# Attention scores from high and low parts in three passes, and the place where the next pair's weights are split

## What is computed

```python
q_lat = jnp.einsum('bthn,lhn->bthl', q_nope, w_uk)
...
s = (jnp.einsum('bqhl,bkl->bhqk', ql, ckv) + jnp.einsum('bqhr,bkr->bhqk', qr, krope))
s = s.astype(jnp.float32) * ATTN_SCALE
mask = (qp[:, None] // CHUNK) >= k_chunk[None, :]
p = jax.nn.softmax(jnp.where(mask, s, -jnp.inf), axis=-1).astype(ckv.dtype)
return jnp.einsum('bhqk,bkl->bqhl', p, ckv)
```

## Time and profile before

| what | value |
|---|---|
| median of 3 runs | 1476.83 us (1472.91 to 1477.15) |
| profiled execution, its own time | 1476.03 us |
| its span, first to last instruction | 1474.0 us |
| TensorE matmul busy | 1278.2 us (87%) |
| VectorE busy | 532.4 us (36%) |
| ScalarE busy | 457.4 us (31%) |
| granted TensorE clock, mean | 0.936 of full speed |

### The profile page before, as it was taken

One profiled execution on the slowest core, in us unless ns is written; L12 is line 12 of the kernel. 1 busy time (PEld: TensorE's weight loads), 2 busy tenths in 40 slices (PEclk: granted clock), 3 DMA queues, 4 the chain that ended last, 5 costly groups with the idle time before them and its releaser, 6 DMA issues.

```text
span 1474.0 us, 22958 instructions
## 1 busy us (share of the span) xinstructions
PE 1278.2 (87%) x8602; PEld 706.5 (48%) x8603; DVE 532.4 (36%) x1057; ACT 457.4 (31%) x713; POOL 32.7 (2%) x40
## 2 busy tenths in 40 slices
PE   6999999999999988888887887788788888887785
PEld 4999999887767733232222222222232233222221
DVE  4335446275664342323222222232213232322233
ACT  5432334245443223232232222222222223222223
POOL 1000000000100000000000000000000000000000
PEclk9999999999999989999898899899889999998898
DMA  9554551132363479999999999999999999999996
GB/s 324 145 172 141 165 170 40 35 109 79 116 196 140 174 296 426 429 433 431 430 433 431 432 434 429 432 434 429 433 434 388 429 435 430 434 431 429 434 431 261
DMA packets 71112, 474.45 MB, mean 322 GB/s; under 512 B 9676, under 2 KB 46800, under 8 KB 56480
## 3 DMA queue, kind: packets, MB, share of 16 engines
q1 hardware_dynamic: 70144, 472.35, 78.5%
q0 software_dynamic: 688, 1.43, 0.3%
q10 hardware_dynamic: 240, 0.09, 0.0%
HBM read 470.49 MB, written 3.38 MB: 321 GB/s over the span
## 4 chain that ended last, share of the span: by engine, by line
PE 63%; DMA 26%; DVE 5%; issue 3%; ACT 3%; DVEq 0%; ACTq 0%; SPq 0%
DMA ring<-in_w_down 16%; PE ps L991 11%; PE ps L1010 8%; PE ps L679 5%; PE ps L680 5%; PE ps L681 5%; DMA gate_b<-in_w_up 4%; PE ps L965 4%; DVE hreg L1742 3%; PE ps L997 2%; DMA gate_b<-in_w_down 2%; DMA ring<-in_w_up 2%; PE ps L843 2%; PE ps L844 2%; PE ps L845 2%
## 5 line engine op out<-in xcount | busy, mean ns | idle before, releaser
L1742 DVE TENSOR_TENSOR hreg<-ps,hreg 128x512 f32<-128x512 f32 x264 | 160.9, 682 | 205.9 <-PE ps L1017 205.9
L991 PE MATMUL ps<-ring,cq 128*32 128x512 f32 x1600 | 185.0, 603 | 22.9 <-DVE hreg L1742 17.3
L1746 DVE TENSOR_TENSOR work<-work,ps 128x128 f32 x33 | 9.5, 288 | 449.9 <-PE ps L997 449.9
L679 PE MATMUL ps<-xT_hi,w_hi 128*128 128x320 f32 (+1 forms) x528 | 164.9, 312 | 0.6 <-DVE w_lo L1437 0.6
L680 PE MATMUL ps<-xT_lo,w_hi 128*128 128x320 f32 (+1 forms) x528 | 164.0, 311 | 0.0
L681 PE MATMUL ps<-xT_hi,w_lo 128*128 128x320 f32 (+1 forms) x528 | 163.9, 310 | 0.0
L1010 PE MATMUL ps<-ring,work 128*32 128x512 f32 x768 | 129.3, 835 | 20.6 <-DMA ring<-in_w_down 20.6
L1017 PE MATMUL ps<-krt,const 32*128 32x512 f32 x528 | 102.7, 626 | 29.7 <-ACT krt L1383 29.7
L991 PEld LDWEIGHTS ps<-ring,cq 128*32 128x32 f32 x1600 | 51.9, 111 | 134.5 <-issue 127.2
L1437 DVE TENSOR_TENSOR w_lo<-ring,w_hi 128x1024 fp32r<-128x1024 f32 (+1 forms) x66 | 76.8, 1205 | 107.6 <-ACT w_hi L1125 107.6
L1125 ACT CAST w_hi<-ring 128x1024 fp32r<-128x1024 f32 (+1 forms) x66 | 65.2, 1033 | 145.8 <-PE ps L681 145.8
(11 more groups left out here) (308 smaller groups left out, 1635.5 us busy)
## 6 DMA issues: line engine op xcount, KB each, us to landing
ring<-in_w_up SPq DMA_DIRECT2D x23, 4096.0 KB, 32.7
ring<-in_w_down SPq DMA_DIRECT2D x23, 4096.0 KB, 33.9
ring<-in_w_gate SPq DMA_DIRECT2D x23, 4096.0 KB, 32.3
ring<-in_w_in SPq DMA_DIRECT2D x32, 1024.0 KB, 8.2
gate_b<-in_w_up SPq DMA_DIRECT2D x8, 4096.0 KB, 31.8
gate_b<-in_w_down SPq DMA_DIRECT2D x7, 4096.0 KB, 33.5
gate_b<-in_w_gate SPq DMA_DIRECT2D x7, 4096.0 KB, 32.3
ring<-in_w_o SPq DMA_DIRECT2D x16, 1024.0 KB, 7.3
```

The costliest lines, as they stand in the source:

```text
L679: pe.matmul(out, hi, xT_hi[:, c, :], start=c == 0, stop=False)
L991: last = pe.matmul(ps[r:r + B, bank, :], x[:, k % 4, k // 4, :], w[:, k, :], start=k < 4, stop=k >= KC - 4)
L1742: dve.tensor_tensor(h, ps[:, COMB_BANKS[u], :], h, ALU.add).then_inc(comb_added, 1)
```

## The change

The scores are computed from parts as well. ScalarE writes the high parts of queries and keys straight from PSUM (`q_hi`, `k_hi`), VectorE the low parts (`q_lo`, `k_lo`), and the bank is drained by VectorE. The rotated queries and the shared rotated keys are split too (`krt_hi`, `krt_lo`, once). A group of scores has six fp32r passes: three with 128 rows, three with 64. The parts take the place of the two buffers, so that queries and keys of one pair at a time are held. The splits of the next pair's weights move: on ScalarE into `queries(p)`, behind the copies of all four key results, and on VectorE to the end of `keys(p)`.

```diff
@@ -110,7 +110,7 @@
     jobs += [("ulast", "act")]
 
     def pair_jobs(p):
-        return ([(f"qr{p}", "act")] + [(f"q{2 * p + i}", "act") for i in range(2)]
+        return ([(f"qr{p}", "act")] + [(f"q{2 * p + i}", "dve") for i in range(2)]
                 + [(f"K{2 * p}_0", "dve"), (f"qrot{p}", "dve"), (f"K{2 * p}_1", "dve")]
                 + [(f"K{2 * p + 1}_{s}", "dve") for s in range(2)])
 
@@ -185,11 +185,14 @@
         assert nc.sbuf_base == ring_at + 4 * (SLOTS * SLOT + 6 * D + KC * T)
         ckv = sb("ckv", [P, LC, KEYS])
         cq = sb("cq", [P, LC, T])
+        krt_at = nc.sbuf_base
         krt = sb("krt", [P, KEYS])
+        assert nc.sbuf_base == krt_at + 4 * KEYS
         const = sb("const", [P, C_ALL])
         par = sb("par", [P, P_ALL])
         ones = sb("ones", [P, P])
         work = sb("work", [P, 4960])
+        work_at = nc.sbuf_base - 4 * 4960
         small = sb("small", [P, 64])
         tables = sb("tables", [1, 4, NE], I32)
 
@@ -251,8 +254,12 @@
         par_rows = work[0:P_ALL, 1280:1280 + P]
         vals = hreg[:, 0:5 * CH].rearrange("p (k v) -> p k v", k=5)
 
-        qt = r2[:, 0:1920].rearrange("p (b i t) -> p b i t", b=2, i=3)
-        kt = r2[:, 1920:4224].rearrange("p (b i k) -> p b i k", b=2, i=2)
+        q_hi = nc.alloc_sbuf_tensor_at("q_hi", [P, 3, T], F32R, offset=r2_at)
+        q_lo = nc.alloc_sbuf_tensor_at("q_lo", [P, 3, T], F32R, offset=r2_at + 4 * 960)
+        k_hi = nc.alloc_sbuf_tensor_at("k_hi", [P, 2, KEYS], F32R, offset=r2_at + 4 * 1920)
+        k_lo = nc.alloc_sbuf_tensor_at("k_lo", [P, 2, KEYS], F32R, offset=r2_at + 4 * 3072)
+        krt_hi = nc.alloc_sbuf_tensor_at("krt_hi", [P, KEYS], F32R, offset=work_at + 4 * 2560)
+        krt_lo = nc.alloc_sbuf_tensor_at("krt_lo", [P, KEYS], F32R, offset=krt_at)
         qraw = r2[:, 4224:4544]
         att_a = r2[:, 4544:4864]
         att_b = r2[:, 4864:5184]
@@ -330,6 +337,8 @@
         cq_hi_ready, cq_lo_ready = sem("cq_hi_ready"), sem("cq_lo_ready")
         wq_hi_ready, wq_lo_ready = sem("wq_hi_ready"), sem("wq_lo_ready")
         wk_hi_ready, wk_lo_ready = sem("wk_hi_ready"), sem("wk_lo_ready")
+        q_hi_ready, k_hi_ready, rope_hi_ready, rope_lo_ready = sem("q_hi_ready"), sem("k_hi_ready"), sem("rope_hi_ready"), sem("rope_lo_ready")
+        krt_hi_ready, krt_lo_ready = sem("krt_hi_ready"), sem("krt_lo_ready")
         s_ones, first_half = sem("s_ones"), sem("first_half")
         xT_hi_ready = sem("xT_hi_ready")
         w_hi_ready, w_lo_ready = sem("w_hi_ready"), sem("w_lo_ready")
@@ -785,14 +794,19 @@
 
             def scores(h):
                 p, i = h // 2, h % 2
-                q, k = qt[:, p % 2], kt[:, p % 2]
-                pe.wait_ge(q_ready, p + 1)
+                pe.wait_ge(krt_lo_ready, 1)
+                pe.wait_ge(rope_lo_ready, p + 1)
                 pe.wait_ge(drained["dve"], drain_count[f"K{h}_1"])
-                pe.wait_ge(drained["act"], drain_count[f"q{h}"])
+                rows = slice(64 * i, 64 * i + 64)
 
                 def score(out, t0, tn, k0, kn):
-                    pe.matmul(out, q[:, i, t0:t0 + tn], k[:, i, k0:k0 + kn], start=True, stop=False)
-                    return pe.matmul(out, q[64 * i:64 * i + 64, 2, t0:t0 + tn], krt[64 * i:64 * i + 64, k0:k0 + kn], start=False, stop=True)
+                    t, k = slice(t0, t0 + tn), slice(k0, k0 + kn)
+                    pe.matmul(out, q_hi[:, i, t], k_hi[:, i, k], start=True, stop=False)
+                    pe.matmul(out, q_hi[:, i, t], k_lo[:, i, k], start=False, stop=False)
+                    pe.matmul(out, q_lo[:, i, t], k_hi[:, i, k], start=False, stop=False)
+                    pe.matmul(out, q_hi[rows, 2, t], krt_hi[rows, k], start=False, stop=False)
+                    pe.matmul(out, q_hi[rows, 2, t], krt_lo[rows, k], start=False, stop=False)
+                    return pe.matmul(out, q_lo[rows, 2, t], krt_hi[rows, k], start=False, stop=True)
 
                 b = claim(pe, f"S{h}a")
                 score(b[:, 0:128], 0, 128, 0, 128)
@@ -1220,6 +1234,8 @@
                     conv_square(NCH - 2)
                     conv_square(NCH - 1)
             keys_hi(0)
+            act.wait_ge(ulast_ready, 1)
+            act.copy(krt_hi[:, :], krt[:, :]).then_inc(krt_hi_ready, 1)
             act.wait_ge(ssq_full, 3)
             root_of("conv", ps[:, SSQ_BANK, 0:T], CH)
             act.wait_ge(psum_full, full("ulast"))
@@ -1232,7 +1248,17 @@
                 drain("qr", act.copy(qraw, bank(f"qr{p}")[:, 0:T]))
                 for i in range(2):
                     act.wait_ge(psum_full, full(f"q{2 * p + i}"))
-                    drain("q", act.copy(qt[:, p % 2, i, :], bank(f"q{2 * p + i}")[:, 0:T]))
+                    act.copy(q_hi[:, i, :], bank(f"q{2 * p + i}")[:, 0:T]).then_inc(q_hi_ready, 1)
+                for i in range(2):
+                    for s, (k0, kn) in enumerate(((0, 256), (256, 320))):
+                        act.wait_ge(psum_full, full(f"K{2 * p + i}_{s}"))
+                        act.copy(k_hi[:, i, k0:k0 + kn], bank(f"K{2 * p + i}_{s}")[:, 0:kn]).then_inc(k_hi_ready, 1)
+                        if i == 0 and s == 1:
+                            act.wait_ge(q_ready, p + 1)
+                            act.copy(q_hi[:, 2, :], att_a).then_inc(rope_hi_ready, 1)
+                if p + 1 < H // 2:
+                    queries_hi(p + 1)
+                    keys_hi(p + 1)
 
             def exps(h):
                 i, pr = h % 2, pb[h % 2]
@@ -1273,8 +1299,6 @@
                     act.copy(o_hi[:, v % 4], o_raw(v)).then_inc(o_hi_ready, 1)
 
             queries(0)
-            queries_hi(1)
-            keys_hi(1)
             for p in range(H // 2):
                 exps(2 * p)
                 exps(2 * p + 1)
@@ -1282,9 +1306,6 @@
                     act.wait_ge(normed, 2 * LC + NCH)
                 if p + 1 < H // 2:
                     queries(p + 1)
-                if p + 2 < H // 2:
-                    queries_hi(p + 2)
-                    keys_hi(p + 2)
                 mix_hi(NCH + 2 * p)
                 mix_hi(NCH + 2 * p + 1)
                 if p == 1:
@@ -1552,20 +1573,29 @@
                 link(dve.memset(mx[k], 0.0))
                 link(dve.memset(sm[k], 1.0))
             keys_lo(0)
+            dve.wait_ge(krt_hi_ready, 1)
+            dve.tensor_tensor(krt_lo[:, :], krt[:, :], krt_hi[:, :].bitcast(F32), ALU.subtract).then_inc(krt_lo_ready, 1)
             scale_chunks(3, [mix[:, 8 + c, :] for c in range(NCH)], P_CO)
 
             def keys(p):
+                for i in range(2):
+                    h = 2 * p + i
+                    dve.wait_ge(q_hi_ready, h + 1)
+                    drain("q", dve.tensor_tensor(q_lo[:, i, :], bank(f"q{h}")[:, 0:T], q_hi[:, i, :].bitcast(F32), ALU.subtract))
                 for i in range(2):
                     for s, (k0, kn) in enumerate(((0, 256), (256, 320))):
                         name = f"K{2 * p + i}_{s}"
-                        dve.wait_ge(psum_full, full(name))
-                        drain(name, dve.tensor_copy(kt[:, p % 2, i, k0:k0 + kn], bank(name)[:, 0:kn]))
-                        if i == 0 and s == 1 and p + 1 < H // 2:
-                            queries_lo(p + 1)
-                            keys_lo(p + 1)
+                        dve.wait_ge(k_hi_ready, 4 * p + 2 * i + s + 1)
+                        drain(name, dve.tensor_tensor(k_lo[:, i, k0:k0 + kn], bank(name)[:, 0:kn], k_hi[:, i, k0:k0 + kn].bitcast(F32), ALU.subtract))
+                        if i == 0 and s == 1:
+                            dve.wait_ge(rope_hi_ready, p + 1)
+                            dve.tensor_tensor(q_lo[:, 2, :], att_a, q_hi[:, 2, :].bitcast(F32), ALU.subtract).then_inc(rope_lo_ready, 1)
                         if i == s == 0:
                             dve.wait_ge(drained["act"], drain_count[f"qr{p}"])
-                            rotate(qt[:, p % 2, 2, :], qraw, bank(f"qrot{p}")[:, 0:T], att_a, att_b, f"qrot{p}").then_inc(q_ready, 1)
+                            rotate(att_a, qraw, bank(f"qrot{p}")[:, 0:T], att_a, att_b, f"qrot{p}").then_inc(q_ready, 1)
+                if p + 1 < H // 2:
+                    queries_lo(p + 1)
+                    keys_lo(p + 1)
 
             def mix_low(v):
```

## The result

| | before | after |
|---|---|---|
| median of 4 runs each | 1474.87 us (1471.31 to 1477.15) | 1502.45 us (1500.66 to 1507.78) |
| ratio, 95% interval | 1 | 1.0196 [1.0178, 1.0215] |
| span of the profiled execution | 1474.0 us | 1500.9 us |
| granted TensorE clock, mean | 0.936 | 0.924 |

The sign is as predicted, the size is not: +27.6 us where +10.2 was forecast. The waits of TensorE came out within about 0.2 us of the timetable. What was missed lies in the clock.

The account below looks back on a forecast made before the run. Bound taken: the attention pairs' chain of TensorE work, carried one to one to the end. Scores -0.8, first pair +0.9, two rounds +6.4, last +0.35, clock +3.4 made +10.2 us: 1486.5 us, range 1478 to 1492.

Parts of the forecast that it names:

- the timetable: TensorE, VectorE and ScalarE over pair 1, read from the trace before: when each step runs and where new steps must fit.
- The gaps: TensorE before the first attend, rounds of pairs 1 and 2: 3.2 us more wait each, 6.4 us together.
- first pair: TensorE ahead of the first pair's scores: waits 0.9 us for the parts on VectorE; bounds 0 and 1.5 us.
- last round: Pair 3, no weights following: last key bank's copy, subtraction and probs_T end 0.35 us behind TensorE's transposes.
- The scores: Scores on TensorE: six fp32r passes a group, 3.36 us a head instead of 3.46; eight heads save 0.8 us.
- rival 1: 48 changes of rows on TensorE free in fp32r: -9.4 us instead of -0.8, sum +1.6, 1478 us; chance 0.20.
- The 128-column pass: fp32r score pass absent from the trace: taken as 0.11 us from the nearest fp32 pass, upper bound 0.21.
- rival 3: Scores: the 128-column fp32r pass costs 0.21 us, +4.8 us on top, 1491 us; chance 0.11.
- The excess in fp32: Score matmuls cost more than elsewhere, 0.20 us (0.14 at 64 weight columns), laid on changes between 128 and 64 rows.
- The clock: TensorE behind the two rounds' gaps: two falls to half clock at 1.7 us each, 3.4 us; at most 2.7 each.
- rival 2: No clock fall, the gap lying between dense stretches: sum +6.9 us, 1483 us; chance 0.15.
- What was priced at nothing: Second key bank's wait for the query drain, lost double buffer, and later ScalarE and VectorE work: claimed free.

Follow-up runs that it names:

- e6_fp32_order: The kernel before with only its six fp32 score matmuls a head reordered, two changes of row count instead of six: 1471.91 us, 0.9979 of before.
- e3_fill: The kernel after with unread matmuls filling TensorE's waits, ahead of the first pair's scores and of the attends in two rounds: 1478.26 us, 1.0044 of before.
- e8_fill_one_round: The kernel after with unread matmuls only ahead of the first scores and in pair 1's round, pair 2's gap open: 1493.77 us, 1.0131 of before.
- e9_dense_behind: The kernel after, first wait filled, both gaps open, 24 unread dense fp32r passes behind each gap ahead of the attends: 1491.61 us, 1.0126 of before.
- e2_late_fp32: The kernel before with its fp32 scores, only the next weights' splits moved behind the last key result: 1502.65 us, 1.0206 of before.
- e5_ahead: The kernel after with the weights of pairs 2 and 3 split a round ahead, rotated shared keys split earlier, same pass order: 1474.16 us, 0.9993 of before.
- e1_early: The kernel after with the next pair's weights split earlier, low parts where the kernel before had them: 1495.13 us, 1.0155 of before.
- e4_snake: The kernel after with every second score group taking its 64-row passes first, 6 changes of row count a pair, not 12: 1491.07 us, 1.0128 of before.
- e7_fill_three: As the kernel after with filled waits, but three unread matmuls instead of four in each of the two gaps: 1479.13 us, 1.0047 of before.

## Why the prediction was right in sign and wrong in size

- **The gaps**: right. 3.6 us predicted, 3.81 measured in the same two rounds, from the same releaser; first pair 0.9 against 0.83, last round 0.35 against 0.47.
- **The scores**: right in kind. 3.36 us a head predicted, 3.21 measured, 3.46 before, so eight heads save 2.0 us and not 0.8. A change of row count is not free in fp32r (rival 1 falls) and costs 0.16 us. The 128-column pass took the 0.11 that was chosen (rival 3 falls). The excess in fp32 was laid wholly on the change of rows; e6_fp32_order shows that only a part of it is.
- **All terms but the clock**: -0.8 + 0.9 + 6.4 + 0.35 = +6.85 predicted, +6.56 at the landmark of e3_fill. With measured sizes: -2.0 + 0.83 + 2 x 3.40 + 0.47 = +6.1. The near agreement is in part luck: the saving was 1.2 us too small, the two gaps 0.4 us too short.
- **The clock**: the step that failed. It put "1.7 us for a fall; I take two falls, 3.4 us", with an upper bound of 2.7 a fall. Measured: 23.2 us. That a gap drops the clock was right (rival 2, no fall, is out), but the term was mis-sized in both factors. A fall behind a 3.81 us gap cost 8.5 and 8.8 us in the kernel after and 9.8 us in e8_fill_one_round, five to six times the price. And there were three: the first pair fell too, behind 0.83 us of idleness, where none was counted, for 5.9 us. Of these 3.3 us were lost up to the start of the next queries at 318.07 (22.96 against 19.69 us from the first query pass in e3_fill), the rest while the dense query passes were bringing the clock back, until 323.8.
- **Why it was mis-sized**: the 1.7 us came from the L991 row: 16 dense fp32 matmuls of 512 columns (the 32 are their passes) behind a gap of 1.71 us, and the clock is back at 548.9 us, before they end. I carried the duration of the low stretch over from there to a place where attends and scores follow; there it lasts 20.5 us. e9_dense_behind puts dense work at this place and the clock returns in 4.7 and 5.9 us. The bound "twice as long" was a guess, and the trace of before had a row against it: behind the gap of 2.23 us in the earlier trace rows the clock was low not for the 2 us of the earlier trace rows alone but for 10:

```profile
532.00:542.00 10.00, 10.00 (x44) 3.82 (x43) 5.04 (x21) 0.00 (x0) 0.00 (x0) 0.50 1.00 427
```

- **What was priced at nothing** (the drains moved to another engine, single buffers, the copies behind on both queues) cost at most the 0.4 us between +6.1 and +6.56, less than the landmark can show.

The place of the splits makes the loss, not the passes: e2_late_fp32 has the move alone and is as slow, e5_ahead has the passes with the splits out of the way and is as fast as before. The two don't simply add up. In the kernel after one of the three falls, the first pair's, comes with the wait for the score parts, which e2 doesn't have, while e2's two falls cost 20.7 us against 17.2. And the passes with the low parts where they were before still lose 1.55% (e1_early), since a gap of 2.22 us is left.

Open: why the first pair falls. After and e1_early fall there, with the wait of 0.83 us and six changes of rows a head; e4_snake, with the same wait and fewer changes, doesn't, nor does e5_ahead, with six changes and no such wait. In these profiles it fell only where both were present; each is one execution, and where the line runs was not measured. Open too: which of the attends and the scores holds the clock low, and the 3 us behind the landmark in e8.

## What to carry to other kernels

A wait on TensorE has two prices: its own length, and what the clock takes from everything behind it until dense work has brought it back. Price the second from a place with the same kind of work behind the gap; here 6.8 us of added waiting in two rounds drew 17.2 us after it, and 0.83 us ahead of the first scores drew 5.9. Before moving work, look at what stands behind it in each queue: splits put behind the copies that TensorE waits for, a round ahead, made the same change cost nothing; and if a wait can't be moved, a few matmuls into a spare bank, whose results nobody reads, took back 23.2 of 29.7 us.

Order passes so that the row count changes seldom: two changes a head instead of six were worth 0.5% in fp32r and 0.2% in fp32.

## What was unexpected of the hardware

- After 2.22 to 3.81 us without TensorE work the clock went to 0.50 and stayed there for 17 to 24 us, mostly continuous attends and scores, until dense query passes had run again; 1.04 us left it at 1.00 (e7_fill_three).
- A wait of 0.83 us was followed by a fall to 0.50 about 2 us into the sparse score passes, and by none when the same passes had fewer changes of row count (e4_snake).
- A change between 128 and 64 rows costs more in fp32r (0.16 us) than in fp32 (0.12 us), so the three-pass form has more to gain from a good order: 2.59 against 2.97 us a head in the same order, where in the old order it is 3.21 against 3.46.
